# Attention core of a two-block network: a unit's transposes and the scores two units ahead change places on TensorE, and a maximum and a scaling on VectorE

## The chip, the core and the metric

The kernel runs on one core of one Trainium2 chip. The metric is the device time of one execution in microseconds (us). The core has a matrix engine (TensorE, in the rows PE for matmuls and PEld for the loads of the stationary operand), VectorE (DVE), ScalarE (ACT), GpSimd (POOL) and SyncE (SP), whose queue issues nearly all loads of weights. Each engine takes its instructions in the order in which the program lists them, and the engines wait for each other by semaphores.

## The reference

The program computes two blocks of a network on 256 tokens of width 1024: first a block with convolution, recurrence, cross-attention and 32 experts, then a block of five feed-forward stages with an attention mixer and a convolution mixer among them. The change lies in the attention mixer alone, between its projections and its output matrix:

```python
# n: 8 heads of 64, windowed with a bias, 256 own and 256 context keys in one softmax
s = concatenate([where(mask, q @ k_band + bias, NEG_INF), q @ k_ctx]); p = softmax(s)
a = p @ v
# d: 4 heads with two score maps each (m = 0, 1), 512 keys
s = einsum('bqhmd,bkhmd->bhmqk', q * 64 ** -0.5, k); p = softmax(s)
dd = (p[:, :, 0] - lam * p[:, :, 1]) @ v
y = concatenate([a, rmsnorm(dd, g) * (1 - lam_init)]) @ w_out
```

Everything is float32.

## The kernel before

The attention core is cut into 16 units, numbered 0 to 15 here (list UNITS, L382). An n unit is one windowed head for all 256 queries. A d unit is one differential head for 128 queries, with its two score maps. Both have two score tiles of 128 queries by 512 keys. The order of the units is n n d n d n d n d n d d d d n n. So there are 8 of each kind; units 10 to 13 are four d units in a row, elsewhere in the middle the kinds alternate. A unit goes through these steps:

- scores S (att_score, L1683, TensorE): two score tiles into two of the four banks of `hi`, those of even units into banks 0 and 1, those of odd units into 2 and 3. It waits until the exponentials of the unit two before it have been taken (`na_e`), since they read the same banks. An n unit also adds its bias by matmuls.
- maximum M (att_max, L2357, VectorE): row maximum of both tiles (L2361), and its negative multiple (L2362), signalled by `na_nm`.
- exponentials X (att_exp, L968, ScalarE): two activations from `hi` into `ap_`, which also sum the rows (L973). `ap_` is a part of `scratch`, again two tiles for even and two for odd units.
- scaling P (att_scale, L2364, VectorE): reciprocal of the sums (L2369), then the tiles times it (L2372 for n; L2374 and L2375 for d), signalled by `na_p`.
- transposes T (att_turn, L1701, TensorE, instructions at L1709): 8 transposes for n, 4 for d, from `ap_` into `lo` banks 0 and 1. It waits for `na_p` and signals `na_t`.
- copy C (att_copy, L977, ScalarE): the transposed tile from `lo` to `apt`, which the rows call `ht` (L982 for n, L984 for d), signalled by `na_pt`.
- values V (att_value, L1714, TensorE): the product with the values, into `lo` bank 2 or 3. It waits for `na_pt`. The first unit of an n pair or of a d head also waits until the result of the pair or head before has been copied out (`na_o`, `df_o`).
- result copy O (att_out, L2377, VectorE, L2382 for n and L2385 for d): after every second n unit and every second d unit. It waits for the values (`na_pv`).

All matmuls go through one helper line, L1069: S writes `hi`, and reads `scratch` (queries and keys of n units), `side,mats` (bias) or `ring` (d units); V writes `lo`, and reads `ht,scratch` (n) or `ht,ring` (d).

The order on each engine is written out by hand. TensorE does S(0), S(1), and then for every i: T(i), S(i+2), V(i). ScalarE does X(0), X(1), and then C(i), X(i+2) up to i = 13, then C(14), the rounding of a piece of output weights, a square, a table load, another rounding and C(15). VectorE does M(0), M(1), P(0), and then for every i: P(i+1), O(i-1), M(i+2). Before the core come the projections, behind it the product with the output matrix and three more stages of feed-forward kind, whose weights the queue of SyncE loads as units of a ring of buffers come free.

Of the kernel before, what the change touches and what calls it, by code (L numbers as in the profile page):

```python
# [107 lines left out]
def program(nc, x_in, mem, norm_mix_g, w_in, conv_w, conv_b, conv_ln_g, conv_ln_b, conv_w_out, hgrn_lb_logits,  # L108
# [6 lines left out]
    with ctx:  # L115
# [17 lines left out]
        with ExitStack() as between:  # L133
            _, _, back_r, _, y_split = (
                between.enter_context(nc.sbuf_tensor(name, shape, F32R))
                for name, shape in (("until_ht", [P, KC, 2, T]), ("until_back", [P, 5376]), ("back_r", [P, T]), ("until_y", [P, 512]),
                                    ("y_split", [P, 2, D])))
        with ExitStack() as between:
            _, hi_r, _, ring_r, _, side_r, gate_r = (
                between.enter_context(nc.sbuf_tensor(name, shape, F32R))  # L140
                for name, shape in (("until_hi", [P, 8192]), ("hi_r", [P, 2 * D]), ("until_ring", [P, 8192]), ("ring_r", [P, RING, UNIT]),
                                    ("until_side", [P, TT * D]), ("side_r", [P, 2, TT * D]), ("gate_r", [P, D])))
# [218 lines left out]
        def first_of(m):  # L361
# [20 lines left out]
        UNITS = (("n", 0, 0), ("n", 1, 0), ("d", 0, 0), ("n", 2, 0), ("d", 0, 1), ("n", 3, 0), ("d", 1, 0), ("n", 4, 0),  # L382
                 ("d", 1, 1), ("n", 5, 0), ("d", 2, 0), ("d", 2, 1), ("d", 3, 0), ("d", 3, 1), ("n", 6, 0), ("n", 7, 0))
# [207 lines left out]
        def _(act):  # L591
# [220 lines left out]
            def round_piece(q):  # L812

                for n, _, _ in source(q):
                    wait_unit(act, n)
                if q >= SLOTS:
                    act.wait_ge(piece_done, q - SLOTS + 1)
                parts = source(q)
                for n, w, k in parts:
                    act.activation(wp[:, q % SLOTS, 0, k:k + w.shape[1], :], w, ACT.Copy).then_inc(piece_hi, 2 // len(parts))  # L820
# [246 lines left out]
        def _(pe):  # L1067
            def mm(dst, lhsT, rhs, start=True, stop=True, **kw):
                return pe.matmul(dst, lhsT, rhs, start=start, stop=stop, **kw)  # L1069
# [613 lines left out]
            def att_score(i):  # L1683

                kind, h, t = UNITS[i]
                b = 2 * (i % 2)
                if i == 1:
                    pe.wait_ge(at_math, 4)
                if kind == "d" and (h, t) == (0, 0):
                    pe.wait_ge(at_rope, 5)  # L1690
                if i >= 2:
                    pe.wait_ge(na_e, 2 * (i - 1))
                for k in range(2):
                    if kind == "n":
                        mm(hi[:, b + k, :], (qo if h % 2 else qe)[:, h // 2, k * P:k * P + P], kaT[:, h // 2, :], True, False)
                        ins = mm(hi[:, b + k, 0:T], flip8, bias[:, 2 * h + k, :], False, True)
                    else:
                        ins = mm(hi[:, b + k, :], (qbo if k else qbe)[:, h, t * P:t * P + P], kbT[:, h, :])
                ins.then_inc(na_s, 1)

            def att_turn(i):  # L1701

                kind, _, _ = UNITS[i]
                b = 2 * (i % 2)
                pe.wait_ge(na_p, 2 * (i + 1))
                for t in range(TT if kind == "n" else 1):
                    for c in range(4):
                        at = c * T + t * P if kind == "n" else c * P
                        ins = pe.transpose(lo[:, at // 512, at % 512:at % 512 + P], ap_[:, b + t, c * P:c * P + P], ident)  # L1709
                        if i == len(UNITS) - 2 and t + c == 0:  # L1710
                            ins.then_inc(unit_used[(U_ATT + 4) % RING], 1)
                ins.then_inc(na_t, 1)

            def att_value(i):  # L1714

                kind, h, t = UNITS[i]
                pe.wait_ge(na_pt, i + 1)
                if kind == "n":
                    if h >= 2 and h % 2 == 0:
                        pe.wait_ge(na_o, h // 2)  # L1720
                    at = HD * (h % 2)
                    for c in range(4):
                        ins = mm(lo[at:at + HD, 2, 0:T], va[:, c, h * HD:h * HD + HD], apt[:, c, :], c == 0, c == 3, tile_position=(0, at))
                else:
                    if h and t == 0:
                        pe.wait_ge(df_o, h)
                    for c in range(4):
                        ins = mm(lo[:, 3, t * P:t * P + P], vb[:, c, h * P:h * P + P], apt[:, c, t * P:t * P + P], c == 0, c == 3)
                ins.then_inc(na_pv, 1)
# [1 line left out]
            att_score(0)  # L1731
            att_score(1)
            for i in range(len(UNITS)):
                att_turn(i)
                if i + 2 < len(UNITS):
                    att_score(i + 2)
                if i == len(UNITS) - 1:
                    pe.wait_ge(rms_sq, 5)
                    for b in range(2):
                        ins = mm(hi[:, 2 + b, :], means[:, 1, :], dsq[:, 2 * b:2 * b + 2, :])  # L1740
                    ins.then_inc(rms_ms, 1)
                att_value(i)
# [44 lines left out]
        def _(dve):  # L1787
# [569 lines left out]
            def att_max(i):  # L2357

                b = 2 * (i % 2)
                dve.wait_ge(na_s, i + 1)  # L2360
                link(dve.tensor_reduce(small[:, 56 + b:58 + b], hi[:, b:b + 2, :], AX.X, ALU.max))  # L2361
                ts(small[:, 48 + b:50 + b], small[:, 56 + b:58 + b], -HD ** -0.5, None, ALU.mult).then_inc(na_nm, 1)  # L2362

            def att_scale(i):  # L2364

                b = 2 * (i % 2)
                r = small[:, 76 + b:78 + b]
                dve.wait_ge(na_e, 2 * (i + 1))
                link(dve.reciprocal(r, small[:, 52 + b:54 + b]))  # L2369
                if UNITS[i][0] == "n":  # L2370
                    for k in range(2):
                        ts(ap_[:, b + k, :], ap_[:, b + k, :], r[:, k:k + 1], None, ALU.mult).then_inc(na_p, 1)  # L2372
                else:
                    link(ts(ap_[:, b + 1, :], ap_[:, b + 1, :], r[:, 1:2], lam, ALU.mult, ALU.mult))  # L2374
                    stt(ap_[:, b, :], ap_[:, b, :], r[:, 0:1], ap_[:, b + 1, :], ALU.mult, ALU.subtract).then_inc(na_p, 2)  # L2375

            def att_out(i):  # L2377

                kind, h, t = UNITS[i]
                if kind == "n" and h % 2:  # L2380
                    dve.wait_ge(na_pv, i + 1)
                    dve.tensor_copy(mergeT[:, h // 2, :], lo[:, 2, 0:T]).then_inc(na_o, 1)  # L2382
                if kind == "d" and t:
                    dve.wait_ge(na_pv, i + 1)
                    dve.tensor_copy(dO[:, h, :], lo[:, 3, 0:T]).then_inc(df_o, 1)  # L2385
# [2 lines left out]
            att_max(1)  # L2388
            att_scale(0)
            for i in range(len(UNITS)):  # L2390
                if i + 1 < len(UNITS):
                    att_scale(i + 1)
                if i:
                    att_out(i - 1)
                if i + 2 < len(UNITS):
                    att_max(i + 2)

            def merged_lo(n, chunks):
                dve.wait_ge(at_mhi, n)
# [31 lines left out]
            for c in range(KC):  # L2431
                i = 3 * c
# [111 lines left out]
```

## Time and profile before

| | |
|---|---|
| median of three runs | 2290.53 us |
| lowest and highest run | 2283.6 and 2293.57 us |
| span of the profiled execution, from its first to its last instruction | 2285.4 us |
| mean granted TensorE clock | 0.989 of full speed |
| TensorE busy with matmuls | 2180.2 us |
| VectorE busy | 1230.4 us |
| ScalarE busy | 869.6 us |
| attention core, from the first maximum to the start of C(15) | 1477.8 to 1554.6 us |

The profile tells no time of the profiled execution other than its span; its span lies 5.1 us under the median of the runs. Times inside the kernel are counted from the start of the span. Busy times are shares of the whole; what the attention core waits for has to be read from its own stretch.

### The profile page before, as it was taken

To read this page: it belongs to the slowest core of one execution; us is meant where nothing else is said; L and a number is where in the kernel's file an instruction comes from. 1 tells how busy PE (TensorE), PEld (TensorE's weight loads), DVE (VectorE), ACT (ScalarE), POOL (GpSimd) and SP (SyncE) were. 2 spreads that over 40 slices of the span, in tenths; PEclk is the share of its full clock that TensorE was granted. 3 is DMA by queue.
4 is the path that set the end of the run, shared out by engine and by line. 5 is a ranking of instruction groups with operands and counts; after the bars stand their busy time and mean duration, and the time that the engine had idled before them with its cause. 6 is when DMAs were issued, how large, how long until landed. Compare 5 with 4: busy or idle time off the path is not lost.

```text
span 2285.4 us, 31138 instructions
## 1 busy us (share of the span) xinstructions
PE 2180.2 (95%) x12406; PEld 1664.9 (73%) x12406; DVE 1230.4 (54%) x2046; ACT 869.6 (38%) x1456; POOL 26.1 (1%) x38
## 2 busy tenths in 40 slices
PE   7999999899999999899999999999999999999998
PEld 6787668654444444588888888757888888888887
DVE  1276234431111111277777774466777777887776
ACT  1102134321111111265464452246554645555444
POOL 1000000010000000000000001000000000000000
PEclk9999999989999999999999999999999999999999
DMA  9988785369999999945554455104465544555351
GB/s 365 401 332 332 295 304 191 136 242 404 430 427 429 428 428 429 383 167 201 175 177 157 149 213 147 46 1 147 148 221 166 179 163 159 182 192 169 115 189 38
DMA packets 205504, 540.30 MB, mean 236 GB/s; under 512 B 7358, under 2 KB 120600, under 8 KB 193096
## 3 DMA queue, kind: packets, MB, share of 16 engines
q1 hardware_dynamic: 202488, 529.59, 61.6%
q0 software_dynamic: 2192, 6.57, 1.0%
q10 hardware_dynamic: 704, 2.47, 0.3%
q8 instruction: 83, 1.36, 0.2%
q14 instruction: 37, 0.30, 0.0%
HBM read 537.56 MB, written 1.05 MB: 236 GB/s over the span
## 4 chain that ended last, share of the span: by engine, by line
PE 44%; DVE 3%; ACT 2%; issue 1%; DVEq 0%; ACTq 0%
PE lo L1069 28%; PE hi L1069 16%; ACT scratch L973 1%; DVE small L2361 1%; DVE scratch L2197 0%; DVE wp L2180 0%; DVE scratch L2375 0%; PE lo L1709 0%; ACT L846 0%; DVE scratch L2372 0%; DVE scratch L2374 0%; ACT xs L829 0%; ACT wp L820 0%; ACT scratch L866 0%; DVE small L2362 0%
## 5 line engine op out<-in xcount | busy, mean ns | idle before, releaser
L1069 PE MATMUL lo<-xs,wp 128*128 128x512 f32 x3904 | 692.0, 339 | 11.7 <-DVE wp L2180 8.5
L1069 PEld LDWEIGHTS lo<-xs,wp 128*128 128x128 f32 x3904 | 597.6, 189 | 104.7 <-issue 13.0
L820 ACT ACTIVATE wp<-ring 128x1024 fp32r<-128x1024 f32 (+1 forms) x500 | 404.2, 832 | 309.8 <-PE hi L1069 179.9
L2180 DVE TENSOR_TENSOR wp<-ring,wp 128x1024 fp32r<-128x1024 f32 (+1 forms) x500 | 459.9, 940 | 3.6 <-ACT wp L820 3.5
L1069 PE MATMUL hi<-hs,wp 128*128 128x512 f32 x2016 | 370.3, 342 | 3.4 <-DVE hs L2429 3.2
L1069 PE MATMUL lo<-ring,scratch 128*64 128x512 f32 x1536 | 336.0, 593 | 27.9 <-DMA ring<-in_moe_w_up_dram 16.3
L1069 PEld LDWEIGHTS hi<-hs,wp 128*128 128x128 f32 x2016 | 311.0, 189 | 50.3 <-DVE hs L2429 3.6
L1069 PEld LDWEIGHTS lo<-ring,scratch 128*64 128x64 f32 x1536 | 129.2, 137 | 223.7 <-issue 209.7
L1069 PE MATMUL lo<-ht,ring 128*128 128x256 f32 (+1 forms) x640 | 137.1, 374 | 4.3 <-DVE ring L2385 1.6
L1069 PEld LDWEIGHTS lo<-ht,ring 128*128 128x128 f32 x640 | 118.4, 193 | 26.1 <-ACT ht L984 4.8
L2225 DVE TENSOR_REDUCE scratch<-lo 128x256 f32<-128x512 f32 x110 | 76.0, 691 | 76.8 <-PE lo L1069 76.7
L2143 DVE TENSOR_TENSOR scratch<-scratch,lo 128x512 f32<-128x512 f32 x16 | 17.4, 1086 | 184.0 <-PE lo L1069 184.0
L2239 DVE SCALAR_TENSOR_TENSOR x<-hi,mod,x 128x256 f32<-128x256 f32 x112 | 54.1, 483 | 76.1 <-PE hi L1069 75.6
L841 ACT ACTIVATE scratch<-lo 128x256 f32<-128x256 f32 x110 | 42.1, 383 | 137.0 <-PE lo L1069 137.0
L2221 DVE TENSOR_TENSOR scratch<-lo,scratch 128x256 f32<-128x256 f32 x110 | 46.7, 424 | 80.1 <-ACT scratch L841 79.8
L2151 DVE SCALAR_TENSOR_TENSOR y_split<-lo,small,y_split 128x512 fp32r<-128x512 f32 x32 | 22.6, 746 | 119.3 <-ACT y_split L801 119.3
L793 ACT ACTIVATE scratch<-lo 128x512 f32<-128x512 f32 x16 | 9.6, 597 | 194.7 <-PE lo L1421 194.7
L1069 PEld LDWEIGHTS lo<-scratch,side 128*128 128x128 f32 x544 | 63.4, 192 | 2.0 <-issue 0.7
L1069 PE MATMUL lo<-scratch,side 128*128 128x128 f32 x544 | 63.5, 275 | 0.0
L801 ACT ACTIVATE y_split<-lo,small 128x512 fp32r<-128x512 f32 x32 | 20.3, 684 | 113.0 <-PE lo L1069 113.0
L2111 DVE TENSOR_TENSOR scratch<-lo,desc 128x512 f32<-128x512 f32 x34 | 23.5, 692 | 68.3 <-PE lo L1069 68.3
L791 ACT ACT_TABLE_LOAD x16 | 20.5, 1283 | 103.9 <-PE lo L1069 103.9
(416 smaller groups left out, 2242.5 us busy)
## 6 DMA issues: line engine op xcount, KB each, us to landing
ring<-in_mod_w_dram SPq DMA_DIRECT2D x72, 1024.0 KB, 13.7
ring<-in_moe_w_up_dram SPq DMA_DIRECT2D x32, 2048.0 KB, 17.3
ring<-in_moe_w_down_dram SPq DMA_DIRECT2D x32, 2048.0 KB, 13.2
ring<-in_moe_w_gate_dram SPq DMA_DIRECT2D x31, 2048.0 KB, 15.8
ring<-in_ffn_w_gate_dram SPq DMA_DIRECT2D x55, 1024.0 KB, 5.7
ring<-in_ffn_w_up_dram SPq DMA_DIRECT2D x55, 1024.0 KB, 9.0
ring<-in_ffn_w_down_dram SPq DMA_DIRECT2D x50, 1024.0 KB, 9.9
ring<-in_w_in_dram SPq DMA_DIRECT2D x20, 1024.0 KB, 12.3
```

The lines of the kernel that those rows point to most:

```text
L791: act.activation(ex_sg, lo[:, 0, :], ACT.Silu).then_inc(ex_sgd, 1)
L820: act.activation(wp[:, q % SLOTS, 0, k:k + w.shape[1], :], w, ACT.Copy).then_inc(piece_hi, 2 // len(parts))
L841: act.activation(sg[:, s % 2], lo[:, 2 * (s % 2), T:2 * T], ACT.Copy).then_inc(g_half, 1)
L973: act.activation(ap_[:, b + k, :], hi[:, b + k, :], ACT.Exp, scale=HD ** -0.5, bias=small[:, 48 + b + k:49 + b + k], accum_out=small[:, 52 ...
L1069: return pe.matmul(dst, lhsT, rhs, start=start, stop=stop, **kw)
L2111: tt(hg[:, 4 * j:4 * j + 4, :], lo[:, 2 + j, :].rearrange("p (c s) -> p c s", c=4), moe_gain[:, 4 * j:4 * j + 4].unsqueeze(2).broadcast_to ...
L2151: stt(y_lo, lo[:, 2 + h, :], wcol, y_hi.bitcast(F32), ALU.mult, ALU.subtract).then_inc(ex_ylo, 1)
L2180: tt(wp[:, q % SLOTS, 1, k:k + w.shape[1], :], w, wp[:, q % SLOTS, 0, k:k + w.shape[1], :].bitcast(F32), ALU.subtract).then_inc(piece_lo, ...
L2221: tt(sg[:, s % 2], lo[:, 2 * (s % 2), 0:T], sg[:, s % 2], ALU.add).then_inc(g_sum, 1)
L2225: dve.tensor_reduce(ub[:, s % 2], both_halves(2 * (s % 2) + 1), AX.X, ALU.add).then_inc(u_sum, 1)
L2239: stt(dst[:, d], hi[:, d % 4, 0:T], g[:, d:d + 1], dst[:, d], ALU.mult, ALU.add).then_inc(ev_half, 1)
L2361: link(dve.tensor_reduce(small[:, 56 + b:58 + b], hi[:, b:b + 2, :], AX.X, ALU.max))
```

## The change

The two loops change their order and nothing else. On TensorE the loop becomes S(i+2), T(i), V(i). On VectorE it becomes M(i+2), P(i+1), O(i-1). No instruction is added or removed, and the waits inside the steps stay as they are. The order on ScalarE isn't touched.

```diff
             att_score(0)
             att_score(1)
             for i in range(len(UNITS)):
-                att_turn(i)
                 if i + 2 < len(UNITS):
                     att_score(i + 2)
+                att_turn(i)
                 if i == len(UNITS) - 1:
                     pe.wait_ge(rms_sq, 5)
                     for b in range(2):
@@
             att_max(1)
             att_scale(0)
             for i in range(len(UNITS)):
+                if i + 2 < len(UNITS):
+                    att_max(i + 2)
                 if i + 1 < len(UNITS):
                     att_scale(i + 1)
                 if i:
                     att_out(i - 1)
-                if i + 2 < len(UNITS):
-                    att_max(i + 2)
```

## Rows read from the trace of the kernel before

**Rows 1.** Page: busy us of each engine, share of the span, instructions.
```profile
PE 2180.2 (95%) x12406; PEld 1664.9 (73%) x12406; DVE 1230.4 (54%) x2046; ACT 869.6 (38%) x1456; POOL 26.1 (1%) x38
```

**Rows 2.** Waits in 1477.8 to 1551: total us, times, longest us.
```profile
ACT scratch L973 <- DVE small L2362: 41.2, 16, 5.7
DVE small L2369 <- ACT scratch L973: 21.7, 15, 1.5
```

**Rows 3.** Chain of waits, X(5) to X(6): start us, us, what.
```profile
1502.91 1.46 ACT scratch L973 x4
...
1504.39 0.18 DVE small L2369
...
1504.60 0.88 DVE scratch L2372 x2
1505.48 1.18 DVE small L2361
...
1506.89 1.46 ACT scratch L973 x4
```

**Rows 4.** Timeline, TensorE: S(5), V(3), T(4), S(6), V(4), T(5), S(7): start us, us, what.
```profile
1498.47 1.02 PE L1069 MATMUL hi<-scratch 128*128 128x512 f32 x2
...
1501.14 1.94 PE L1069 MATMUL lo<-ht,scratch 128*64 128x256 f32 x8
...
1503.01 0.66 PE L1709 MATMUL lo<-mats,scratch 128*128 128x128 f32 x4
...
1503.51 1.88 PE L1069 MATMUL hi<-ring 128*128 128x512 f32 x4
...
1505.23 0.94 PE L1069 MATMUL lo<-ht,ring 128*128 128x128 f32 x7
...
1506.12 1.04 PE L1709 MATMUL lo<-mats,scratch 128*128 128x128 f32 x8
...
1506.99 1.02 PE L1069 MATMUL hi<-scratch 128*128 128x512 f32 x2
```

**Rows 5.** Timeline where TensorE and a copy wait for each other: C(0); C(8), V(8).
```profile
1484.81 1.02 ACT L982 ACTIVATE ht<-lo 128x1024 f32<-128x1024 f32 x1 [1.56 <-PE lo L1709]
...
1521.74 0.59 ACT L984 ACTIVATE ht<-lo 128x512 f32<-128x512 f32 x1
...
1522.39 0.97 PEld L1069 LDWEIGHTS lo<-ht,ring 128*128 128x128 f32 x8 [0.61 <-ACT ht L984]
```

**Rows 6.** Timeline of the start: end of X(0), T(0), S(2).
```profile
1480.47 0.20 ACT L973 ACTIVATION_READ_ACCUMULATOR scratch<-hi,small 128x1 f32 x1
...
1482.80 1.97 PE L1709 MATMUL lo<-mats,scratch 128*128 128x128 f32 x8 [2.50 <-DVE scratch L2372]
...
1484.56 2.65 PE L1069 MATMUL hi<-ring 128*128 128x512 f32 x4
```

**Rows 7.** Windows: length, busy us of PE, PEld, DVE, ACT, POOL, then granted clock, DMA.
```profile
1482.80:1484.50 1.70, 1.70 (x8) 1.70 (x9) 1.05 (x3) 0.45 (x2) 0.00 (x0) 0.50 0.00 0
...
1540.00:1544.00 4.00, 2.35 (x16) 1.82 (x15) 2.95 (x6) 1.15 (x4) 0.00 (x0) 1.00 0.00 0
```

**Rows 8.** Timeline of d units on VectorE: reciprocal of unit 6, O(4), M(7).
```profile
1508.37 0.17 DVE L2369 RECIPROCAL small<-small 128x2 f32<-128x2 f32 x1 [1.51 <-ACT scratch L973]
...
1509.89 0.42 DVE L2385 COPY ring<-lo 128x256 f32<-128x256 f32 x1
1510.23 1.21 DVE L2361 TENSOR_REDUCE small<-hi 128x2 f32<-128x1024 f32 x1
```

**Rows 9.** Timeline of the end: V(12), T(14), X(15), C(14), C(15).
```profile
1541.93 1.13 PE L1069 MATMUL lo<-ht,ring 128*128 128x128 f32 x8 [1.65 <-DVE ring L2385]
...
1546.81 1.04 PE L1709 MATMUL lo<-mats,scratch 128*128 128x128 f32 x8
...
1548.92 1.02 ACT L982 ACTIVATE ht<-lo 128x1024 f32<-128x1024 f32 x1
...
1554.62 1.02 ACT L982 ACTIVATE ht<-lo 128x1024 f32<-128x1024 f32 x1
```

## The prediction

> **What bounds the kernel now.** I read the busy times of the whole page first: TensorE is busy for 95% of the span [rows 1], so outside the attention core nothing moves unless TensorE does. Nothing there is touched. The core is 77 of the 2285 us, and the rest of the text is about it.
>
> Then the waits inside the core. ScalarE's exponentials wait 41.2 us in total for the negative maximum, and VectorE's reciprocal waits 21.7 us for the exponentials [rows 2]. So the two engines wait for each other in turns. The chain of waits shows how [rows 3]: X(5) takes 1.48 us until the reciprocal starts, P(5) with its reciprocal 1.09 us (1504.39 to 1505.48), the maximum of unit 6 until its exponentials 1.41 us (to 1506.89). The sum is 3.98 us for an n unit. A d unit has the longer scaling, 1509.89 - 1508.37 = 1.52 us from the reciprocal to the next instruction, which makes 4.41 us, and a result copy before the next maximum costs 0.34 us more [rows 8]. A copy comes with every second unit. A pair of an n and a d unit thus needs 3.98 + 4.41 + 0.34 = 8.73 us on this loop.
>
> Last, TensorE in the same stretch, from one first matmul to the next [rows 4]: S(5) 2.67, V(3) 1.87, T(4) 0.50, S(6) 1.72, V(4) 0.89, T(5) 0.87, together 8.52 us for a pair, with not a gap. So TensorE is only 2 to 3% from being the bound in the alternating part. Only for d units in a row, with 0.5 + 1.72 + 0.89 = 3.1 us on TensorE against 4.5 or more on the loop, does it stand idle.
>
> **What the new VectorE order does.** M(i+2) no longer stands behind P(i+1), so the maximum can run while ScalarE takes X(i+1). This cuts the 8.73 us loop. VectorE's own work for a pair is 2 x 1.41 for maxima, 1.09 + 1.52 for scalings and 0.34 for the result copy, 5.8 us, and no bound. The price of the new order: P(i+1) and O(i-1) are now queued behind M(i+2), which waits for S(i+2). I come back to that.
>
> **What the new TensorE order does.** Scores two units ahead need the exponentials of unit i only, and not its scaling. But before, S(i+2) lay between T(i) and V(i), and V(i) waits for C(i), which waits for T(i). S (1.72 or 2.6 us) was the cover of this copy. Now V(i) follows T(i) directly, and no matmul can pass it: TensorE stands idle from the end of the last transpose until the copy is done, in every unit. Working it out from rows:
> - n unit: T(i) needs 1.04 us until its last transpose ends [rows 4] and 0.04 until the copy starts (1482.80 + 1.97 to 1484.81 at the start [rows 5, 6]), so 1.08; the copy 1.02 us [rows 5]; 0.06 until the next load on TensorE (1521.74 + 0.59 to 1522.39 [rows 5]). Together 2.16 us from T(i) to V(i) where the transposes alone take 0.87: 1.29 us are added.
> - d unit: 0.66 + 0.04 + 0.59 + 0.06 = 1.35 us, and V(i), with a first load that waits, about 1.00 us instead of 0.89. Against 0.49 + 0.89 = 1.38 us before it is 2.35: 0.97 us are added.
>
> A pair now takes S 2.6 + 1.72, T to V 2.16 + 1.35, V 1.87 + 1.00 = 10.7 us on TensorE, against 8.73 on the old loop. The new bound is later than the one removed.
>
> The Trainium skill has a rule that speaks against the change too. Its page "Perfetto Trace Analysis" (section Optimizing Tensor Performance, Matmuls) wants independent groups to rotate through PSUM banks, so that the evacuation of one overlaps the matmuls of the next. Before the change the row of C(8) shows such an evacuation under S(10). The page gives no price; by the rows the lost overlap is the 1.29 and 0.97 us above.
>
> **The sum, as a walk along TensorE.** X(0) ends at 1480.67 [rows 6], so S(2) starts at 1480.70 instead of 1484.56. T(0) still waits for P(0), until 1482.80: 0.40 us of idle time. From S(2) to the start of T(14) TensorE does:
> - the scores of units 2 to 15, six n at 2.6 and eight d at 1.72: 29.4 us (2.6 is just under the row's 2.67, since the next load is another; the longer one would add 0.4),
> - T, copy and V of units 0 to 13, six n at 2.16 + 1.87 = 4.03 and eight d at 2.35: 24.2 + 18.8 = 43.0 us,
> - the 0.40 us at the start.
>
> Two places add the price of the VectorE order. V(12) begins a new d head and waits for O(11). In the queue of VectorE O(11) now stands behind M(14) and P(13), and M(14) waits for S(14). From the last score of S(14): 0.16 until it is complete (1.88 on the row of S(6) against 1.72 to the next matmul [rows 4]), 1.41 for M, 1.52 for P, 0.42 for the copy, 3.5 us, less T(12) of 0.49: a gap of 3.0 instead of 0.86, 2.1 us more. The other result copies are an iteration or more ahead of their readers. And T(14) waits for P(14) behind M(15): 0.16 + 1.41 + 1.09 = 2.66 us after S(15), against 2.35 for the T and V of unit 13 that lie in between: 0.3 us.
>
> 29.4 + 43.0 + 0.4 + 2.1 + 0.3 = 75.2, so T(14) starts at 1480.7 + 75.2 = 1555.9, where it was 1546.81 [rows 9].
>
> **The clock.** After a gap of 2.50 us on TensorE the transposes of T(0) and then S(2) ran at half the clock, 1.2 GHz [rows 6, 7]: from T(0) to S(2) it was 1.76 us instead of 0.87, and S(2) took 2.65 instead of the 1.88 of S(6), so 1.7 us lost. After V(12)'s old gap of 1.65 us it stayed at 2.4 GHz [rows 7, 9]. The change removes the first gap (its loss is in the old time and not in my walk) and makes one of 3.0 us before V(12). I take the drop there as likely, at 1.2 us; its bounds are 0 (it falls and recovers inside the gap, or not at all) and 1.7. The new gaps of 0.7 to 1.1 us are under the one that left the clock up. T(14) then starts at about 1557.1.
>
> **The end.** C(14) starts 1.08 us after T(14), at 1558.2; it was 1548.92, held up there by X(15). From C(14) to C(15) ScalarE needs at least 5.6 us of its own (1548.92 to 1554.62 less about 0.1 us [rows 9]), so C(15) starts at 1563.8 instead of 1554.62: 9.2 us later. What follows hangs on C(15). Loads of weights wait for the ring buffer that T(14) frees and shift along with it; the new order moves no load past another. TensorE is the bound of the later stages, which can't give the delay back. I take 9.3 us. Against the profiled execution that is a span of 2285.4 + 9.3 = 2294.7; the span lies 5.1 us under the median, and I carry this over: 2290.5 + 9.3 = 2299.8 us.
>
> **Rivals.**
> 1. *The exposed copies cost half as much.* TensorE's starts and ends in a profile are modelled, and a part of the 1.29 and 0.97 us could be an artefact. The six n and eight d units add 7.7 + 7.8 = 15.5 us in the walk; half of it gone leaves about +2 us, 2292. Against it speaks the wait of V(8), which was already released by its copy in this way [rows 5]. Chance 0.13.
> 2. *Faster: the copies stay covered and only the loop of ScalarE and VectorE shortens.* For this, V(i) would have to find its copy done. The walk without the 15.5 us puts T(14) at 1540.4, and the end 7.5 us earlier, with no clock loss 8.7: 2282 us. It decides where a copy ends before TensorE has got through T(i), and C(i) reads what T(i) writes. The time is also that of a change that did what its order is meant for, and is still within 0.5%, since TensorE is so close behind the loop. Chance 0.03.
> 3. *Slower by more: the clock falls in many gaps.* At each of the six n units before unit 14 TensorE is idle for about 1.1 us within 6.7. If each such gap cost 1.7 us as the first one of before did, 10 us come on top: 2310. It decides from a gap length between 1.65 and 2.50 us on the rows, if gap length alone counts. The Trainium skill, "TensorE: Matmul & The Clock Gate" (section on the second failure mode, cycling through PSUM queues), reports such oscillation from micro-idle times between groups; no row of this kernel shows it. Chance 0.08.
> 4. *VectorE stands in more places.* P(i+1) behind M(i+2) could hold up T(i+1) in other units too, if PSUM reads or waits are longer than I took them. In the walk, followed unit by unit, P(i) is done between 0.9 us (unit 11) and 2.6 us before T(i) can start in the middle of the core. At 0.5 us for each unit it is 2303 to 2307. Chance 0.08.
>
> **How the numbers follow.** The forecast has a chance of 0.68, with its own range of 2294 to 2305: the clock's bounds of -1.2 and +0.5, some 0.2 us for each of fourteen units, and 2 us for the run. A measurement of this kernel can tell about 0.5%, 11.5 us, from no change; the bound is at 2302. Of the forecast I put a quarter above it, 0.17, with rival 3 0.08 and rival 4 0.06 of its 0.08: slower 0.31. Faster than 2279 needs more than rival 2 gives: 0.02. The rest is 0.67. The range for 8 in 10 is 2292 to 2307; it leaves out rivals 2 and 3.
>
> **What the profile of the changed kernel would show.** S(2) starts at about 1480.7, before T(0), and the low clock around 1483 is gone. TensorE's loads and matmuls on `ht` are released by L982 and L984 in nearly all 16 units, some 15 us in total. The exponentials' wait for L2362 shrinks far below 41 us, and in its place the copies wait for the transposes at L1709. X(2) starts some 3.8 us earlier, X(5) or X(6) at about the old time, X(14) some 5 us later. V(12) waits for L2385 for about 3 us and the clock dips behind it. C(15) starts near 1564. I'd be wrong if V(i) starts less than 2 us after T(i) in n units, or if the pair takes less than 9 us on TensorE.

## The result and the profile after

The changed kernel takes 2296.11 us, median of six runs (2293.51 to 2299.29); the kernel before, measured in as many, 2285.65 us. The ratio is 1.0045 with an interval of 1.0029 to 1.0061: the change makes the kernel slower by 6.6 to 13.9 us, 10.3 in the middle, against a forecast of 9.3. The profiled executions have spans of 2295.1 and 2285.4 us, 9.7 us apart. From the first maximum to the start of C(15) it is 86.59 us (1478.72 to 1565.31) where it was 76.86 (1477.76 to 1554.62), 9.73 us more. What lies around the core differs by under 1 us in each direction and cancels, so this stretch holds the whole difference. I call it the core's stretch below.

The waits of the changed kernel inside the core (1477.8 to 1560; total us, times, longest us), which answer to [rows 2]:

```profile
DVE small L2361 <- PE hi L1069: 37.5, 15, 5.6
ACT ht L984 <- PE lo L1709: 25.5, 8, 6.4
ACT ht L982 <- PE lo L1709: 16.2, 7, 4.3
...
ACT scratch L973 <- DVE small L2362: 10.3, 10, 5.7
...
PE lo L1069 <- ACT ht L982: 6.7, 6, 1.1
...
PE lo L1069 <- ACT ht L984: 4.8, 7, 0.7
...
PE lo L1069 <- DVE ring L2385: 3.0, 1, 3.0
...
DVE small L2369 <- ACT scratch L973: 0.5, 1, 0.5
```

The old loop no longer sets the pace: the exponentials' wait for the maximum falls from 41.2 to 10.3 us, and the reciprocals' wait for the exponentials from 21.7 to 0.5. But now VectorE and ScalarE wait for TensorE (first three lines), and TensorE waits for the copy in 13 of the 14 units from 0 to 13 (1.1 us each at L982, 0.7 at L984); in unit 12 it waits for a result copy instead. TensorE, which the two others wait for and which itself waits for a copy, sets the pace.

The timeline of TensorE and the copies over one pair, S(5), T(3), C(3), V(3), which answers to [rows 4]:

```profile
1498.65 1.02 PE L1069 MATMUL hi<-scratch 128*128 128x512 f32 x2
...
1501.23 1.04 PE L1709 MATMUL lo<-mats,scratch 128*128 128x128 f32 x8
...
1502.31 1.02 ACT L982 ACTIVATE ht<-lo 128x1024 f32<-128x1024 f32 x1 [2.83 <-PE lo L1709]
...
1503.38 1.94 PE L1069 MATMUL lo<-ht,scratch 128*64 128x256 f32 x8 [1.11 <-ACT ht L982]
```

T to V takes 1503.38 - 1501.23 = 2.15 us where the transposes alone took 0.87 [rows 4]. V(5), one pair on, starts at 1514.09, so a pair takes 10.71 us on TensorE, against 8.52 before.

And the place at V(12), which answers to [rows 9]: the maximum M(14), the reciprocal of P(13) and the result copy O(11) on VectorE, then V(12), S(15), T(13) and T(14) on TensorE:

```profile
1547.39 1.22 DVE L2361 TENSOR_REDUCE small<-hi 128x2 f32<-128x1024 f32 x1 [1.93 <-PE hi L1069]
...
1548.73 0.16 DVE L2369 RECIPROCAL small<-small 128x2 f32<-128x2 f32 x1
...
1550.24 0.41 DVE L2385 COPY ring<-lo 128x256 f32<-128x256 f32 x1
1550.80 1.16 PE L1069 MATMUL lo<-ht,ring 128*128 128x128 f32 x8 [3.01 <-DVE ring L2385]
1551.77 1.90 PE L1069 MATMUL hi<-scratch 128*128 128x512 f32 x2
...
1556.04 0.60 PE L1709 MATMUL lo<-mats,scratch 128*128 128x128 f32 x4
...
1558.71 1.09 PE L1709 MATMUL lo<-mats,scratch 128*128 128x128 f32 x8 [0.22 <-DVE scratch L2372]
```

V(12) waits for the result copy O(11), which VectorE now does behind M(14) and P(13). Behind the gap of 3.01 us S(15) needs 1556.04 - 1551.77 = 4.27 us instead of some 2.58. The windows (length, busy us of PE, PEld, DVE, ACT, POOL, then the granted clock) show why:

```profile
1549.00:1552.00 3.00, 1.20 (x9) 1.23 (x10) 1.55 (x3) 1.30 (x4) 0.00 (x0) 0.96 0.00 0
1552.00:1556.00 4.00, 4.00 (x8) 1.98 (x8) 0.00 (x0) 0.00 (x0) 0.00 (x0) 0.60 0.00 0
```

The granted clock is at 0.60 on average in the second one, at half speed (1.2 GHz) for most of it.

### The profile page after: what moved, and what is told of

Read it like the earlier page. It is cut to its first block and busy times, and to the rows that moved or that the text cites. A ratio compares the mean times of both kernels' runs of the same rounds, so it can differ in the third digit from the quotient of the medians.

```text
span 2295.1 us, 31138 instructions
## 1 busy us (share of the span) xinstructions
PE 2179.0 (95%) x12406; PEld 1666.0 (73%) x12406; DVE 1229.3 (54%) x2046; ACT 869.9 (38%) x1456; POOL 26.0 (1%) x38
## 5 line engine op out<-in xcount | busy, mean ns | idle before, releaser
L1069 PE MATMUL lo<-ht,ring 128*128 128x256 f32 (+1 forms) x640 | 135.4, 371 | 11.2 <-ACT ht L984 4.8
L2143 DVE TENSOR_TENSOR scratch<-scratch,lo 128x512 f32<-128x512 f32 x16 | 17.4, 1088 | 184.1 <-PE lo L1069 184.1
```

What stands on the lines that cost most here:

```text
L2143: tt(ex_h.rearrange("q (f p) -> q p f", f=4), ex_sg.rearrange("q (p f) -> q p f", f=4), lo[:, 1, :].rearrange("q (p f) -> q p f", f=4), AL ...
```

## The experiments

The theory (A): each V waits for its own copy, because the scores that used to cover it now stand in front of the transposes; on top of it come the place at V(12) and the clock behind it. The first rival (B): VectorE's order costs the time, since P and O are queued behind a maximum. The second: the gaps on TensorE are an artefact of modelled ends, or copies count only in part. The eight runs, with the core's stretch from their profiles (each stretch is read from one execution, each ratio from 4 to 12 executions of the variant; an added line shifts the line numbers in the rows behind it by a few):

| run | ratio to before, interval | core's stretch, us | against before |
|---|---|---|---|
| before | 1 | 76.86 | |
| the change | 1.0045 (1.0029 to 1.0061) | 86.59 | +9.73 |
| TensorE's order alone | 1.0021 (1.0007 to 1.0035) | 82.16 | +5.30 |
| VectorE's order alone | 1.0083 (1.0065 to 1.01) | 98.36 | +21.50 |
| change, result copy first | 1.0022 (1.0007 to 1.0037) | 82.61 | +5.75 |
| change, gap at V(12) filled | 1.0038 (1.0024 to 1.0051) | 84.91 | +8.05 |
| change, every copy twice | 1.0128 (1.0108 to 1.0147) | 104.0 | +27.2 |
| before, every copy twice | 1.0014 (1.0002 to 1.0026) | 79.2 | +2.4 |
| V one unit later, two copy buffers | 0.9951 (0.9933 to 0.997) | 68.03 | -8.83 |
| the same, VectorE's old order | 0.9992 (0.998 to 1.0004) | 72.91 | -3.95 |

(With copies taken twice the stretch ends at the first of the two copies of unit 15, 0.92 us before the signalled one.)

### TensorE's order alone

```diff
 # on top of the kernel before
             for i in range(len(UNITS)):
-                att_turn(i)
                 if i + 2 < len(UNITS):
                     att_score(i + 2)
+                att_turn(i)
```

> Only TensorE's order is changed: S(i+2), T(i), V(i); VectorE keeps P(i+1), O(i-1), M(i+2). Theory A (each V(i) waits for its own copy because no scores lie between): the gaps before V stay at about 1.1 us (n) and 0.7 us (d) in units 0 to 13. O(11) stands ahead of M(14) again, so the gap before V(12) is 0.7 instead of 3.0 us and the clock doesn't fall there: of the change's 9.7 us some 2.2 and 1.7 go, and 0.3 at T(14). Span 5.5 to 6 us over before, ratio 1.0025. Rival B (the cost comes from VectorE's order, with P(i+1) and O(i-1) queued behind a maximum that waits for scores): back to the time of before or below, ratio 1.000 or less, since TensorE's order alone only starts scores earlier.

Measured: +5.30 us in the core and a ratio of 1.0021, as theory A has it; back to before, as in rival B, lies outside the interval. The gaps are still there, and the one at V(12) is an ordinary one of a d unit (timeline of this run, TensorE, V(12)):

```profile
1550.21 1.16 PE L1069 MATMUL lo<-ht,ring 128*128 128x128 f32 x8 [0.69 <-ACT ht L984]
```

In this kernel the reciprocals wait 23.0 us for the exponentials and the maxima for the scores only 10.0: the old order of VectorE stands idle in other places than the new one, and nearly to the same end, since TensorE's chain is the longest in both.

### VectorE's order alone

```diff
 # on top of the kernel before
             for i in range(len(UNITS)):
+                if i + 2 < len(UNITS):
+                    att_max(i + 2)
                 if i + 1 < len(UNITS):
                     att_scale(i + 1)
                 if i:
                     att_out(i - 1)
-                if i + 2 < len(UNITS):
-                    att_max(i + 2)
```

> Only VectorE's order is changed: M(i+2), P(i+1), O(i-1); TensorE keeps T(i), S(i+2), V(i). Then P(i+1) waits behind M(i+2) for S(i+2), and T(i+1) follows V(i) at once. By the rows of before T(i+1) waits for what is left of M and P behind V(i): 0.16 + 1.41 + 1.09 or 1.52 less V(i) of 1.87 or 0.89, that is 0.8 to 2.2 us in each of units 1 to 14. Theory A: no cover for the copies is lost, but the two orders need each other; in sum some 23 us over before, ratio 1.010. If VectorE's order by itself were harmless: ratio 0.997 to 1.000.

Measured: +21.50 us in the core, ratio 1.0083. This is the slowest of the orders tried. The scaling P(i+1) that T(i+1) needs is stuck behind a maximum whose scores TensorE does only after T(i). The waits of TensorE's two queues before the transposes of this kernel add up to (view of line L1709: total us, times):

```profile
  DVE scratch L2372: 24.2, 14
  DVE scratch L2375: 22.7, 14
```

Matmuls and weight loads are counted both here; the gaps before the matmuls alone add up to 21.2 us, of which 2.5 are before T(0), as in the kernel before. Its clock fell too, behind the gaps of 2.13 us before T(11) and T(12). The two halves of the change thus aren't a sum: +5.3 and +21.5 by themselves, +9.7 together. The scores ahead are what makes the maximum ahead bearable.

### Result copy first

```diff
 # on top of the change
             for i in range(len(UNITS)):
+                if i:
+                    att_out(i - 1)
                 if i + 2 < len(UNITS):
                     att_max(i + 2)
                 if i + 1 < len(UNITS):
                     att_scale(i + 1)
-                if i:
-                    att_out(i - 1)
```

> The changed kernel, with O(i-1) in front of M(i+2) on VectorE: O(i-1), M(i+2), P(i+1). Theory A with the place at V(12) as its own term: the gap before V(12) falls from 3.0 to 0.7 us, the clock stays at full speed there, the other gaps stay. Span some 6 us over before instead of 9.7, ratio 1.0026. If the 3.0 us gap didn't matter for the end: 9.7 us over before, as the change.

Measured: +5.75 us in the core, 3.98 under the change, and a ratio of 1.0022. One result copy in the wrong place in a queue is worth 4 us, of which 2.3 are the longer gap (3.01 against 0.69 us) and the rest is about the clock's share, which the next run measures. With O(11) out of the way VectorE's new order (82.61 us) is no better than its old one (82.16 us, the run above): as long as TensorE waits for its copies, it gains nothing.

### The gap at V(12) filled

```diff
 # on top of the change
                     ins.then_inc(rms_ms, 1)
+                if i == 12:
+                    keep_busy(lo[:, 1], 4)
                 att_value(i)
```

> The changed kernel with eight matmuls more, as those of keep_busy (128x384 each, four calls), into the idle bank 1 of lo in front of V(12), so that TensorE works through the 3.0 us gap there; by the rows they last about 2.6 us. Theory A with the clock as its own term: the granted clock stays at full speed in the 4 us behind V(12), S(15) takes 2.6 instead of 4.3 us, and the stretch from the first maximum to C(15) falls from 86.6 to about 84.9 us; span 8 us over before instead of 9.7. If the slow S(15) were a cost of something other than the idle gap: no change to 86.6, or longer by what the added matmuls stick out.

Measured: the core's stretch is 84.91 us, 1.68 less than in the change, though eight matmuls were added. Timeline of TensorE, from the filling to S(15) and T(13):

```profile
1553.91 2.75 PE L1069 MATMUL lo<-mats 128*128 128x384 f32 x8
1557.09 1.13 PE L1069 MATMUL lo<-ht,ring 128*128 128x128 f32 x8 [0.43 <-DVE ring L2387]
1558.05 1.02 PE L1069 MATMUL hi<-scratch 128*128 128x512 f32 x2
...
1560.63 0.60 PE L1709 MATMUL lo<-mats,scratch 128*128 128x128 f32 x4
```

and the window behind V(12):

```profile
1557.10:1560.60 3.50, 3.50 (x16) 2.43 (x17) 0.00 (x0) 0.00 (x0) 0.00 (x0) 1.00 0.00 0
```

S(15) takes 2.58 us again, at a granted clock of 1.00. V(12) starts 3.62 us after T(12), as in the change (3.61), so the clock's price is shown apart from the wait for O(11). As a time of the whole kernel the step is too small to tell: 1.0038 and 1.0045 have intervals that overlap. The profiled span, 2301.0 us, is one execution that began its core 6.3 us later than the change's; the stretch is what can be compared.

### Every copy twice, in both kernels

```diff
 # on top of the change, and on top of the kernel before
                 if kind == "n":
+                    act.activation(apt_twin, lo[:, 0:2, :], ACT.Copy)
                     ins = act.activation(apt, lo[:, 0:2, :], ACT.Copy)
                 else:
+                    act.activation(apt_twin[:, :, t * P:t * P + P], lo[:, 0, :].rearrange("p (c n) -> p c n", c=4), ACT.Copy)
```

> The changed kernel with every C done twice (once more into an unused buffer, before the one that is signalled): 0.92 us more in n units, 0.5 us in d units. Theory A: nothing covers a copy, so nearly all of it appears: 7 x 0.92 + 8 x 0.5 = 10.4 us less the 0.5 at V(12), where O(11) is later anyway; from the first maximum to C(15) 96 to 97 us instead of 86.6, and 0.9 more at C(15) itself, span 20 to 21 us over before, ratio 1.009. Rival (copies are half covered): 5 us more than the change, ratio 1.0065.

> The kernel before with every C done twice in the same way. Theory A: S(i+2), 1.7 to 2.7 us, covers the longer copy in the most part, only where d scores cover a copy of 1.94 us some 0.5 us stick out: 1 to 2 us more until C(15) and 0.9 at C(15), span 2 to 3 us over before, ratio 1.001. Rival (the added ScalarE work is itself what costs, covered or not): 10 us over before, ratio 1.0045, as in the changed kernel.

Measured: the same added work on ScalarE costs the kernel before 2.4 us in the core (ratio 1.0014) and the changed one 17.4 us (104.0 - 86.6). In the one the scores cover most of the copy, in the other nothing does: the gap before V grows from 1.11 to 2.03 us in n units and from 0.69 to 1.17 in d units, by as much as the copy does. That rules out the rival of half-covered copies (5 us). But 17.4 is more than the 9.9 that the copies account for, and my expectation of 96 to 97 us missed the 104.0 by 7. The timeline of TensorE in the changed kernel with doubled copies, T(3), V(3), S(6), T(4), V(4):

```profile
1501.49 1.04 PE L1711 MATMUL lo<-mats,scratch 128*128 128x128 f32 x8
1504.55 3.43 PE L1071 MATMUL lo<-ht,scratch 128*64 128x256 f32 x8 [2.03 <-ACT ht L983]
1507.91 2.14 PE L1071 MATMUL hi<-ring 128*128 128x512 f32 x4
1509.88 0.60 PE L1711 MATMUL lo<-mats,scratch 128*128 128x128 f32 x4
1511.65 1.16 PE L1071 MATMUL lo<-ht,ring 128*128 128x128 f32 x8 [1.17 <-ACT ht L986]
```

and the windows in which its clock was low and not, each of 6 us:

```profile
1490.00:1496.00 6.00, 3.97 (x16) 2.00 (x15) 2.33 (x5) 3.27 (x6) 0.00 (x0) 1.00 0.00 0
...
1502.00:1508.00 6.00, 3.97 (x14) 1.92 (x12) 2.45 (x5) 3.27 (x6) 0.00 (x0) 0.74 0.01 3
...
1544.00:1550.00 6.00, 5.03 (x12) 2.45 (x13) 1.27 (x3) 2.25 (x6) 0.00 (x0) 0.72 0.00 0
```

V(3) took 3.36 us (1504.55 to 1507.91) instead of 1.87, at half the clock behind a gap of 2.03 us. A gap of the same length before V(1), in the window from 1490 to 1496, did not lower it. From V(3) to T(4) it is 5.33 us, 1.64 more than in the change, and the same is lost behind the gaps before V(5), V(7) and V(9). Before V(12) the gap is 3.01 us as in the change, but the clock stays low for longer: from V(12) to T(13) it is 6.46 us, 1.22 more than there. These five places add up to 7.8 us, which is the missing 7 us or so: the clock, which my expectation had left out for gaps of 2.0 us. That reading rests on the granted clock; no run here takes the clock's part away from this kernel.

### V one unit later

```diff
 # on top of the change: two copy buffers, apts[i % 2] in att_copy and att_value
-        ap_, apt = part(12288, 4, KEYS), htpart(3072, 4, T)
+        ap_, apts = part(12288, 4, KEYS), (htpart(2048, 4, T), htpart(3072, 4, T))
...
                 b = 2 * (i % 2)
+                if i:
+                    pe.wait_ge(na_pt, i)
                 pe.wait_ge(na_p, 2 * (i + 1))
...
                 if i + 2 < len(UNITS):
                     att_score(i + 2)
                 att_turn(i)
+                if i:
+                    att_value(i - 1)
...
-                att_value(i)
+            att_value(len(UNITS) - 1)
```

T(i) writes the banks of `lo` that C(i-1) reads. V(i-1) used to stand before it and kept it behind that copy; now the added `wait_ge(na_pt, i)` does.

> The changed kernel with V one unit later on TensorE: S(i+2), T(i), V(i-1), and two buffers for the transposed tile (even and odd units), so that C(i) runs while TensorE does V(i-1) and S(i+3). Theory A: the 14 gaps before V are gone, TensorE is busy through the alternating part with a pair at 8.5 us, and T(14) starts some 7 us earlier than in before (by 18 us earlier than in the change). Span 8 us under before, ratio 0.9964. Rival B: VectorE's order is the same as in the change, so the time stays 6 to 10 us over before. If the modelled ends of matmuls mislead and the gaps are no real idle time: the same as the change, ratio 1.004.

> The version with V one unit later and two copy buffers, but with VectorE's old order P(i+1), O(i-1), M(i+2). It tells what VectorE's new order is worth once the copies are covered. Theory A: TensorE is fed by the old loop of VectorE and ScalarE again (8.7 us a pair, 4.4 or more for each of the four d units in a row), so some 4 to 5 us of the 8.8 us gain are lost: from the first maximum to C(15) 72.5 to 73.5 us instead of 68.0, span 4 us under before, ratio 0.998. If only the covered copies mattered: 68 us as with the new order.

Measured: 68.03 us in the core with VectorE's new order, 8.83 under before and 18.56 under the change, and a ratio of 0.9951, 2274.86 us: faster than both kernels. TensorE has no gap in the alternating part, and a pair takes 1504.39 - 1495.82 = 8.57 us (timeline of this run, T(3), V(2), C(3), then the next pair's T(5)):

```profile
1495.82 1.04 PE L1712 MATMUL lo<-mats,scratch 128*128 128x128 f32 x8
1496.69 1.06 PE L1070 MATMUL lo<-ht,ring 128*128 128x128 f32 x8
1496.89 1.02 ACT L983 ACTIVATE ht<-lo 128x1024 f32<-128x1024 f32 x1 [3.05 <-PE lo L1712]
...
1504.39 1.04 PE L1712 MATMUL lo<-mats,scratch 128*128 128x128 f32 x8
```

The copy starts as late behind T as in the change (0.2 us after V(2)'s first matmul), but TensorE has work until it is done. With VectorE's old order in the same version the stretch is 72.91 us, 4.88 more, and the intervals of the two ratios don't overlap (the old order's, 0.998 to 1.0004, doesn't exclude the time of before). TensorE waits there for the exponentials before S(13), S(14) and S(15) (0.49, 1.47 and 0.28 us) and for the scalings before T(14) and T(15):

```profile
PE lo L1712 <- DVE scratch L2378: 3.8, 2, 2.0
```

With the new order the only waits at these places are 1.26 us before T(14) and 0.22 before T(15). So VectorE's new order is worth nearly 5 us once the copies are covered, all of it in the four d units and behind them: in the alternating part a pair takes 8.57 us with either order. In the change, where TensorE waits for its copies, there is no such gain. Rival B is wrong in its sign.

## Why the prediction was right

**The bound of before.** The loop of VectorE and ScalarE was read rightly: with the copies covered, VectorE's new order takes the exponentials' wait for the maximum from 36.6 to 10.3 us. (That it falls in the change too is no proof, since with TensorE's order alone it is 12.3: there TensorE is simply slower.) That TensorE was only 2 to 3% behind the loop is shown by the version with covered copies: its pair of 8.57 us is the 8.52 of the prediction.

**The exposed copies.** T to V in n units was put at 2.16 us and is 2.15. In d units it is 1497.65 - 1496.37 = 1.28 us for the 1.35 that I had, since the last of four transposes ends 0.6 us after the first begins and not 0.66. A pair was put at 10.7 us and takes 10.71. That it fits so well is partly luck: S in d units takes 1.82 us (1494.55 to 1496.37) and not 1.72, and this makes up for the 0.07 of the copy. TensorE's idle time that the profile lays at the copies was expected at 15 us and is 11.5 (6.7 + 4.8 us) up to unit 13, 13.4 with 1.11 before V(14) and 0.77 before V(15); unit 12 is missing in it, and the time in which the last transpose runs out, 0.17 us in a n unit, is counted as busy. Rival 1, copies that cost half as much, is ruled out by the doubled copies and by the version that covers them.

**The place at V(12).** 3.0 us against 3.01. T(14) follows S(15) at 2.66 us by the sum and 1558.71 - 1556.04 = 2.67 us in the profile. The 0.22 us before T(14) is all that TensorE waits for a scaling after T(0), so rival 4 did not happen.

**The clock.** The dip came. I took 1.2 us with bounds of 0 and 1.7; S(15) lost 4.27 - 2.58 = 1.69 us, and filling the gap gave back 1.68. Here the step was under-sized, at my own upper bound. The new gaps of 0.7 to 1.1 us left the clock at full speed, so rival 3 did not happen; the doubled copies show that gaps of about 2.0 us bring it about in some units.

**The start and the end.** S(2) was put at 1480.7. It starts at 1481.77 in an execution whose first maximum is 0.96 us later, at 1480.81 on the old scale. X(2) is 3.9 us earlier by the same scale (3.8), X(5) and X(6) lie within 0.9 us of the old time, X(14) is 4.7 us later (5). T(14) is at 1557.75 on it for the forecast 1557.1, C(15) at 1564.35 for 1563.8. The 0.6 us is the clock's 0.5 and small change. Between C(14) and C(15) ScalarE needs 5.47 us for the 5.6 that I had. I took these from the 5.70 of before, but there C(15) also waited for T(15), and I had overlooked that the clock was low: behind a gap of 2.15 us before V(14), V(14) and T(15) took 4.42 us (1550.00 to 1554.42) instead of the 2.80 of the changed kernel. The window of the kernel before:

```profile
1552.70:1554.40 1.70, 1.70 (x9) 1.69 (x9) 0.00 (x0) 1.61 (x3) 0.00 (x0) 0.51 1.10 347
```

Hidden behind ScalarE's work, this low clock cost the kernel before some 0.2 us only.

**The total.** 9.3 us were forecast and 10.3 (6.6 to 13.9) measured. The predicted time of 2299.8 us lies 3.7 over the measured 2296.11 because it was counted from the median of the first three runs of before, 2290.53, which six runs put at 2285.65, 4.9 us lower; the slowdown being about 1 us larger than forecast took a part of this back. The bound between no change and slower, 0.5% or 11.5 us, is inside the interval, so which side of it the change falls on is open; the sign itself is outside doubt.

**Rival 2**, the copies covered and only the loop shortened, was priced at 8.7 us at best under before and given 0.03 for this change. The version with V one unit later makes its condition true and comes out at 8.83 us in the core, and at 11.2 (7 to 15) in the whole. That the core's figure fits is luck. The walk had no clock loss in it, so its 7.5 us was already the best case, and the 8.7 took the 1.2 us off a second time; it also kept 2.4 us for V(12) and T(14), which that version pays only in part (1.26 us before T(14)).

## What to carry to other kernels

On an engine that works in order, look at what lies between a step and the step that waits for its result from another engine. If work is moved out of there, the full round trip (here 1.08 + 1.02 + 0.06 us in an n unit, of which the transposes' own work is 0.87) is laid open once per iteration, however idle the engine looked elsewhere. To issue work earlier and keep the cover, move the consumer by one iteration too, and pay for it with a second buffer.

In a queue, a step that waits late must not stand ahead of one that somebody needs early: one result copy behind one maximum made 4 us, 1.7 of them by the clock.

## What I had not expected of the hardware

The length of a gap on TensorE doesn't settle by itself whether its clock falls to half. Behind a gap of 2.03 us it did before V(3) of the changed kernel with doubled copies, and did not before V(1). With VectorE's order alone it even stayed up behind the gap of 3.45 us before V(12), as the windows behind it show (1566.8 is the start of V(12); granted clock as before):

```profile
1563.40:1566.80 3.40, 0.00 (x0) 0.02 (x1) 3.09 (x6) 1.45 (x4) 0.00 (x0) 1.00 0.00 0
1566.80:1570.00 3.20, 3.19 (x18) 2.43 (x19) 0.00 (x0) 0.60 (x1) 0.00 (x0) 1.00 0.00 0
```

A short gap isn't safe by itself either. The twelve gaps of 0.69 or 1.11 us before V(0) to V(11) in the change left the clock at 1.00, and so did the 1.65 us before V(12) of the kernel before. But with VectorE's order alone V(14) took 3.46 us instead of 1.87 behind a gap of 1.11 us, which followed one of 1.61 us before T(14):

```profile
1573.47 1.09 PE L1709 MATMUL lo<-mats,scratch 128*128 128x128 f32 x8 [1.61 <-DVE scratch L2372]
1575.67 3.53 PE L1069 MATMUL lo<-ht,scratch 128*64 128x256 f32 x8 [1.11 <-ACT ht L982]
...
1575.60:1576.60 1.00, 0.93 (x3) 0.54 (x4) 0.00 (x0) 1.00 (x3) 0.00 (x0) 0.50 0.89 298
```

Where it fell, that cost TensorE 1.6 to 1.7 us in most places, whether the gap was 1.1 or 3.0 us long, and 2.9 us once (behind V(12)'s gap with doubled copies: 6.46 us from V(12) to T(13), against 3.54 with the gap filled). What decides it stays open.
